# A hybrid encoder layer on one core: the values product of attention turned round in split form, the softmax division moved to GpSimd, scores two tiles ahead, and the heads' share of w_out in PSUM banks of its own

## The reference, cut to what matters

```python
# D_MODEL = 1024, SEQ = 1024, 8 heads x 64, 16 experts
x = LN(x);  proj = x @ w_in
y_hy = hyena(proj)            # 256 channels
y_lr = rglru(proj)            # 256 channels
# MLA, per head h, all 1024 queries and keys (96 = 64 nope + 32 rope channels)
s = (q_nope @ k_nope.T + q_rope @ k_rope.T) * 96 ** -0.5
p = softmax(s, axis=-1)
o = p @ v                     # 1024 x 64 per head, 8 heads: 512 channels
y = concat(rms(y_hy) * g0, rms(y_lr) * g1, rms(o) * g2)
x = LN(alpha * x + y @ w_out)
x = LN(alpha * x + expert_choice_moe(x))   # 16 experts, 128 tokens each
```

## Time and profile before

| what | value |
|---|---|
| runs (three) | 1750.42, 1754.76 (median), 1759.69 us |
| profiled execution, first to last instruction | 1750.5 us |
| busy over the span | PE 1574.6, PEld 1135.9, DVE 1075.2, ACT 757.3, POOL 247.5 us |
| attention, first scores to last values product | about 673 to 955 us |
| mix, from there to its last product | about 955 to 1070 us |
| experts | about 1131 to 1700 us |

### The profile page before, as it was taken

One profiled execution on the slowest core, in us unless ns is written; L12 is line 12 of the kernel. 1 busy time (PEld: TensorE's weight loads), 2 busy tenths in 40 slices (PEclk: granted clock), 3 DMA queues, 4 the chain that ended last, 5 costly groups with the idle time before them and its releaser, 6 DMA issues.

```text
span 1750.5 us, 18114 instructions
## 1 busy us (share of the span) xinstructions
PE 1574.6 (90%) x6806; PEld 1135.9 (65%) x6806; DVE 1075.2 (61%) x1247; ACT 757.3 (43%) x853; POOL 247.5 (14%) x140
## 2 busy tenths in 40 slices
PE   5999989999899998999998997099999999999970
PEld 2444467854334346999897786088888888888760
DVE  6211244441350436667765564779998998998858
ACT  5201100023340313445554234067777777777742
POOL 0400000000000000000000431303223322332214
PEclk9999989999999998999998997599999999999995
DMA  5506000070100000000101335779999999999964
GB/s 193 205 0 222 24 1 1 1 137 24 48 0 0 0 0 24 1 1 25 37 13 53 118 112 196 268 256 373 370 379 379 379 370 379 379 373 376 379 226 180
DMA packets 152864, 284.58 MB, mean 163 GB/s; under 512 B 25268, under 2 KB 35842, under 8 KB 152803
## 3 DMA queue, kind: packets, MB, share of 16 engines
q1 hardware_dynamic: 147043, 262.76, 42.3%
q0 software_dynamic: 4608, 16.78, 3.7%
q10 hardware_dynamic: 1152, 4.19, 0.6%
HBM read 258.54 MB, written 25.17 MB: 162 GB/s over the span
## 4 chain that ended last, share of the span: by engine, by line
PE 80%; DVE 9%; ACT 4%; DMA 4%; issue 2%; POOL 0%; POOLq 0%; ACTq 0%; SPq 0%; DVEq 0%
PE psum L936 15%; PE psum L1239 9%; PE psum L1241 8%; PE psum L1240 8%; PE psum L1126 5%; PE psum L1077 4%; PE psum L971 3%; PE psum L920 3%; DMA arena<-in_exp_w_down 3%; PE psum L1116 3%; PE psum L1185 2%; PE psum L1187 2%; PE psum L1186 2%; PE psum L981 2%; PE psum L982 2%
## 5 line engine op out<-in xcount | busy, mean ns | idle before, releaser
L1658 DVE TENSOR_TENSOR split_at<-arena,split_at 128x2048 fp32r<-128x2048 f32 x188 | 427.6, 2290 | 61.2 <-ACT split_at L819 59.5
L819 ACT ACTIVATE split_at<-arena 128x2048 fp32r<-128x2048 f32 x192 | 367.4, 1916 | 63.6 <-PE psum L1241 54.1
L1239 PE MATMUL psum<-split_at,split_at 128*128 128x512 f32 x768 | 306.2, 399 | 1.4 <-DVE split_at L1664 1.4
L1241 PE MATMUL psum<-split_at,split_at 128*128 128x512 f32 x768 | 300.7, 391 | 0.0
L1240 PE MATMUL psum<-split_at,split_at 128*128 128x512 f32 x768 | 299.8, 390 | 0.0
L936 PE MATMUL psum<-arena 128*128 128x512 f32 (+1 forms) x608 | 265.5, 596 | 3.7 <-DVE arena L1334 3.7
L936 PEld LDWEIGHTS psum<-arena 128*128 128x128 f32 (+1 forms) x608 | 113.3, 187 | 151.4 <-issue 146.8
L1241 PEld LDWEIGHTS psum<-split_at,split_at 128*128 128x128 f32 x768 | 144.7, 188 | 31.3
L1239 PEld LDWEIGHTS psum<-split_at,split_at 128*128 128x128 f32 x768 | 145.0, 189 | 29.8 <-DVE split_at L1664 1.8
L1240 PEld LDWEIGHTS psum<-split_at,split_at 128*128 128x128 f32 x768 | 145.1, 189 | 28.4
L754 ACT ACTIVATE arena<-psum,arena 128x1024 f32<-128x1024 f32 x64 | 71.2, 1113 | 134.4 <-DVE arena L1531 134.3
(11 more groups left out here) (253 smaller groups left out, 2173.2 us busy)
## 6 DMA issues: line engine op xcount, KB each, us to landing
arena<-in_exp_w_gate SPq DMA_DIRECT2D x64, 1024.0 KB, 14.2
arena<-in_exp_w_up SPq DMA_DIRECT2D x64, 1024.0 KB, 14.1
arena<-in_exp_w_down SPq DMA_DIRECT2D x64, 1024.0 KB, 14.3
arena<-in_w_in SPq DMA_DIRECT2D x9, 1024.0 KB, 5.1
arena<-in_x SPq DMA_DIRECT2D x8, 512.0 KB, 4.4
xhat_scratch<-arena SPq DMA_DIRECT2D x8, 512.0 KB, 6.5
arena<-in_w_out SPq DMA_DIRECT2D x8, 512.0 KB, 3.2
arena<-xhat_scratch SPq DMA_DIRECT2D x8, 512.0 KB, 4.8
```

What stands on the lines that cost most here:

```text
L819: a(flat(wsplit[c % WS][0]), wraw[:, c], ACT.Copy).then_inc(s_whi, 1)
L1239: mm(bank(out_bank), src[0][:, k, :], whi[:, k % 4, :], start=(k == 0), stop=False)
L1241: ins = mm(bank(out_bank), src[1][:, k, :], whi[:, k % 4, :], start=False, stop=(k == KT - 1))
L1658: tt(flat(lo), wraw[:, c], flat(hi), ALU.subtract).then_inc(s_wlo, 1)
```

## The change

Four things are changed together.

1. The values product is turned round. Two units make a pair. The turned probabilities are split (ACT copies both banks as the high part, L817; DVE subtracts, L1654) and are now the moving operand, 256 columns wide; the values, split once per head by POOL (`v_split`, high and low side by side, 128 columns), are the weights. Eight products with the high part (`pv_high`, L1225) and eight with the low part (`pv_low`, L1232) give both halves of the answer in one bank, which ACT copies (`o_copy`) and DVE adds (`o_sum`) into a transposed output. The values product is no longer followed by a turn of the outputs.
2. The division by the sum moves ahead of the turn and to POOL: DVE inverts the sum (`sum_inverse`), POOL scales the 128x1024 probabilities (L541), and `probs_turn(n)` waits for that. The subtractions for the heads, for w_out and for the two groups move from DVE to POOL too; for w_out POOL scales (L551) and subtracts (L552).
3. PE makes `scores` two units ahead of the turn, not one.
4. In the mix the heads' share goes to banks 2 and 3 and is normalised when DVE adds it; its sum of squares is made by PE from squares of ACT, four products with a column of ones per tile. The other groups' share goes to banks 0 and 1.

```diff
+            def head_low(h, part):
+
+                pool.wait_ge(s_qkh, 2 * h + 3 + part)
...
+            for n in range(N_UNIT):
+                h, qt = divmod(n, TT)
+                pool.wait_ge(s_rc, n + 1)
+                pool.tensor_scalar(p_at[:, n % 2, :], p_at[:, n % 2, :], rinv[:, n % 2:n % 2 + 1], None, ALU.mult).then_inc(s_ps, 1)
+                if h + 1 < NH and qt in (1, 3):
+                    head_low(h + 1, qt // 2)
+                if h + 1 < NH and qt == 4:
+                    v_split(h + 1)
+                if n in WOUT_AT:
+                    k = WOUT_AT.index(n)
+                    _, lo, hi = wout[k]
+                    pool.wait_ge(s_woh, k + 1)
+                    w = wout_in[:, k % 2, :]
+                    link(pool.tensor_scalar(w, w, par[:, C_GN + k:C_GN + k + 1], None, ALU.mult))
+                    pool.tensor_tensor(lo, w, hi, ALU.subtract).then_inc(s_wol, 1)
+                if n in GROUPS_AT:
...
+                    pool.wait_ge(s_yh, m + 1)
+                    pool.tensor_tensor(y_lo[g][:, c, :], (yT_hy, hs)[g][:, c, :], y_hi32[g][:, c, :], ALU.subtract).then_inc(s_yl, 1)
...
+            probs(0)
+            rotary_high(1)
+            probs(1)
             for n in range(NH * TT):
                 h, qt = divmod(n, TT)
...
+                if n >= 4 and n % 2 == 0:
+                    o_copy(n // 2 - 2)
+                probs_high(n)
+                if n + 2 < N_UNIT:
+                    probs(n + 2)
+                if h + 1 < NH and qt in (0, 2):
                     head_high(h + 1, qt // 2)
                 if n in WOUT_AT:
                     k = WOUT_AT.index(n)
                     act.wait_ge(s_wo[k % 2], 16 * (k // 2 + 1))
                     a(wout[k][0], wout_in[:, k % 2, :], ACT.Copy, scale=par[:, C_GN + k:C_GN + k + 1]).then_inc(s_woh, 1)
...
             def probs_turn(n):
-                pe.wait_ge(s_exp, n + 1)
+                pe.wait_ge(s_ps, n + 1)
...
                     if n:
-                        pe.wait_ge((s_pta, s_ptv)[b], n)
+                        pe.wait_ge(s_ptv, 2 * n + b - 1)
...
+            def pv_high(p):
+
+                h = p // 4
+                pe.wait_ge(s_pta, 2 * p + 2)
...
+                for k in range(KT):
+                    mm(bank(6 + p % 2)[:, 0:256], vs[:, h % 2, k, :], pT_hi[:, p % 2, k, :], start=(k == 0), stop=False)
...
+            for n in range(N_UNIT):
+                if n + 2 < N_UNIT:
+                    scores(n + 2)
+                probs_turn(n)
+                if n >= 2:
+                    (pv_high, pv_low)[n % 2](n // 2 - 1)
...
+            row_max(0)
+            rotary_low(1)
+            row_max(1)
+            sum_inverse(0)
+            for n in range(N_UNIT):
+                if n + 1 < N_UNIT:
+                    sum_inverse(n + 1)
+                if n + 2 < N_UNIT:
+                    row_max(n + 2)
+                if n >= 4 and n % 2 == 0:
+                    o_sum(n // 2 - 2)
+                probs_low(n)
```

More of the change, by code:

```diff
@@ L334, in encoder @@
         N_UNIT = NH * TT
-        WOUT_AT = [TT * h + qt for h in range(3, 7) for qt in (5, 7)]
-        GROUPS_AT = [N_UNIT - 7, N_UNIT - 5, N_UNIT - 3, N_UNIT - 2]
+        SUMS = 10
+        ROOTS = 3
+        N_PAIR = N_UNIT // 2
+        WOUT_AT = [TT * h + qt for h, qt in ((3, 5), (3, 7), (5, 5), (5, 7), (6, 5), (6, 7), (7, 1), (7, 3))]
+        GROUPS_AT = [TT * h + qt for h, qt in ((2, 5), (2, 7), (4, 5), (4, 7))]
         def heads_bank(u):
@@ L460, in _ @@
                 sp.wait_ge(s_acst[i], 16 * TT // 2)
-            for c in range(8, WC):
+            for c in range(7, WC):
                 load_chunk(0, c)
@@ L1171, in _, with mix @@
             pe.wait_ge(s_wol, KT)
-            y = [(group[0][:, c, :], group[1][:, c, :]) for group in (y_hy, y_lru, *y_at) for c in range(2)]
+            pe.wait_ge(s_yl, 4)
+            def mix(b0, k, high, low, first, last):
+                for j in range(2):
+                    out_, cols = bank(b0 + j), slice(HALF * j, HALF * j + HALF)
+                    mm(out_, high, wout[k][0][:, cols], start=first, stop=False)
+                    mm(out_, high, wout[k][1][:, cols], start=False, stop=False)
+                    ins = mm(out_, low, wout[k][0][:, cols], start=False, stop=last)
+                return ins
@@ new lines, in _ @@
+                    for k in range(4):
+                        ins = mix(0, k, y_hi[k // 2][:, k % 2, P * i:P * i + P], y_lo[k // 2][:, k % 2, P * i:P * i + P], k == 0, k == 3)
+                    ins.then_inc(s_mxa, 1)
+                    pe.wait_ge(s_sq, SUMS + i + 1)
+                    if i == 0:
+                        pe.wait_ge(s_ov, N_PAIR)
+                    else:
+                        pe.wait_ge(s_rsd, ROOTS + i)
+                    for c in range(4):
+                        ins = mm(bank(7)[:, i:i + 1], o_sq[:, i % 2, c, :], ones[:, 0:1], start=(c == 0), stop=(c == 3))
@@ L1188, in _ @@
+                    ins.then_inc(s_ssq, 1)
+                    pe.wait_ge(s_ol, i + 1)
+                    if i:
+                        pe.wait_ge(s_mixu, i)
+                    for c in range(4):
+                        ins = mix(2, 4 + c, ya_hi[:, i % 2, c, :], ya_lo[:, i % 2, c, :], c == 0, c == 3)
                     ins.then_inc(s_mix, 1)
@@ new lines, in sum_inverse, with probs_low @@
+                v.reciprocal(rinv[:, n % 2:n % 2 + 1], rsum[:, n % 4:n % 4 + 1]).then_inc(s_rc, 1)
+            def probs_low(n):
+                p = n // 2
+                v.wait_ge(s_pta, n + 1)
+                for b in range(2):
+                    blocks, cols = slice(4 * b, 4 * b + 4), slice(P * (n % 2), P * (n % 2) + P)
+                    tt(pT_lo[:, p % 2, blocks, cols], bank(4 + b).rearrange("p (k q) -> p k q", k=4), pT_hi32[:, p % 2, blocks, cols],
+                       ALU.subtract).then_inc(s_ptv, 1)
```

309 lines of the change are left out of this document (154 added, 155 removed).

## The result

| what | kernel before | changed kernel |
|---|---|---|
| median of the timed runs | 1757.2 us (4 runs, 1750.4 to 1759.7) | 1880.6 us (4 runs, 1879.8 to 1882.1) |
| ratio to before, 95% interval | 1 | 1.0706 (1.0681 to 1.073) |
| profiled span | 1750.5 us | 1877.8 us |
| attention, first scores to last values product | 672.93 to 954.84: 281.9 us | 676.12 to 1074.50: 398.4 us |
| from there to the first top-k instruction | 136.3 us | 144.1 us |

The change made the kernel 7% slower; 1797 us with a range of 1760 to 1838 was predicted. Of the 127.3 us between the two spans, attention has 116.5, the mix 7.9, and 3.2 are a later start of attention. The rest of the kernel is the same to 0.2 us.

What follows compares the result with a forecast made beforehand. Attention was bound by PE; afterwards POOL's in-line waits for ACT would stall PE. From 1750.5: attention +29.4, mix -5.8, clock +21.6 gave 1795.7, stated as 1797 us, range 1760 to 1838.

Steps and rivals of the forecast that it cites:

- POOL's prices: POOL in attention: a 1024-column subtraction takes 2.39 us, the scaling s = 1.2, between a fill's 0.95 and 2.39.
- POOL's own load then fits: Attention, per head: POOL's scalings, subtractions, `v_split` and up to two w_out blocks take 24 of 26 us.
- The rival that was called dear: Attention: POOL's scaling costs as much as a subtraction, 2.39, so 40 us more, 1837; chance 0.10.
- The order on POOL does not fit: Attention: side work waiting for ACT delays the next scaling; a w_out block's ring is 7.07 + 2s; stalls total 91.5 us.
- the 26 places named: Attention stalls: eight w_out blocks at 6.22 us each, four groups at 4.84, 14 next-head splits at 1.59.
- The rival that the stalls are hidden: Attention: scaling runs far enough ahead that PE does not wait; 1683 without stalls and clock loss; chance 0.14, all gains included.
- The unit without side work: Attention: a unit falls from 4.06 to 3.25 us, eight 256-column products taking 0.92; alone, 51 us less.
- the rival that 256 columns gain nothing: Attention: a 256-column product takes 0.23 us, a unit 4.17, total 1821; chance 0.05.
- the rival that DVE and POOL hold each other up: Attention: scalings slow the subtractions by 0.86 per unit, ring 4.04, 40 us more, 1837; chance 0.05.
- The mix: Stage after attention: waits of 7.3 and 5.4 us go, 6.9 for sums of squares come; net -5.8 us.
- The clock: PE in attention: half clock after each of 12 long stalls loses 1.8 us each, +21.6 us.
- The 14 short stalls I take as too short: Attention, next-head splits: these stalls were priced without clock loss; otherwise they would cost 25 us more.

Runs made afterwards that it cites:

- the run without the queue: Changed kernel with POOL's side work of unit n written behind the scaling of unit n + 2, all computation kept: 1782.8 us, 1.0147.
- the repeated scores: Changed kernel in which PE repeats its scores products in units whose turn comes late, so it has work while POOL waits: 1870.8 us, 1.0641.
- 8 columns: Changed kernel with POOL scaling only 8 of the 1024 probability columns per unit, all waits and order kept: 1798.7 us, 1.0236.

## Why the prediction was wrong

The direction and the mechanism were right, and the time was 84 us short. Against the profiled execution (1877.8, predicted 1795.7, 82.1 apart):

- **POOL's prices: this step failed.** "The scaling has one input tensor ... I take s = 1.2, near the fill": it took 2.84, above even the upper bound of 2.39. I took two inputs for the dear end because I thought the price grows with the operands. The runs show that the form of the instruction decides: 2.84 as a scaling by a column, 2.77 by a constant, 1.89 as a two-tensor product with a repeated operand, 2.34 to 2.40 for a subtraction. Why the form with fewer inputs is the dearer one stays open. The scaling stands 34 times in the stalls and once ahead of the first turn: 35 x 1.64 = 57.4 us. With the load, 8 x 2.84 + 2.40 + 2.39 + 1.9 = 29.4 us per head, "POOL's own load then fits" fell as well: it is more than PE's 26, as the run without the queue shows. The Trainium skill (GPSIMD Engine Reference, section 3.1 and section 4.1) led to estimates of 1.54 and 0.85 us; this trace agrees with neither, its 2.84 lies above both. The rival that was called dear was not dear enough.
- **The order on POOL does not fit: right.** The stalls are at the 26 places named, with the releasers named. With s = 2.84 the formula gives 7.07 + 5.68 = 12.75 for a w_out block and the trace 13.39, of which 1.09 is the turn at half clock; for the next head it gives 6.89 + 2.84 = 9.73 and the trace 873.24 - 862.83 = 10.41, with 1.10 for the half clock. The rival that the stalls are hidden did not happen. `v_split`, costed at nothing, stands on the chain in three heads; that is a small part of the rest below.
- **The unit without side work: right.** 3.21 to 3.25; 0.95 for eight products; the rival that 256 columns gain nothing is out. So is the rival that DVE and POOL hold each other up: of the changed kernel's scalings in attention none that stands alone took over 2.86, and the w_out subtractions all took 2.34. DVE's subtractions there read PSUM and SBUF; in attention the slow cases came only in the run with DVE's scaling, which reads SBUF (above).
- **The mix: wrong in sign.** -5.8 was forecast, +7.9 came, 13.7 apart. "POOL's first residual ... is done some 9 us after attention": it was, at 1080.49 + 2.40 = 1082.9, 8.4 after. The step that failed is that I looked at the first tile alone and called the rest hidden: from the second tile on POOL waits for ACT ahead of each residual, up to 11.8 us. With that order turned the stage gives -6.3, so the other parts of the term were good to 0.5 us.
- **The clock: too low, partly shown.** 21.6 was forecast as 12 times 1.8, and the step that failed here is "The 14 short stalls I take as too short". (The prediction speaks of three waits of PE and shows two.) Of the 64 turns 20 ran at half clock: the 12 behind the long stalls, 7 of the 14 behind a next head's split, as the one at 871.26 with 1.98, and the first one. On the chain these 20 have 21.9 us over 0.88 each, and the other products 13.7 over their full-clock durations, together 35.6. What attention has over the sum corrected for the scaling is 29.7 in all, 8.1 more than the forecast 21.6. The chain says that this is mostly clock; the stalls' other links were a little shorter than written down (12.30 in place of 12.75 for a block, without the half clock), and the repeated scores gave back 9.8. A finer split stays open.
- **The start: scatter.** 3.2 of the miss. The kernels of these runs have the same code up to attention and start it anywhere from 672.5 to 677.8; the kernel before starts it at 672.4. The clock ahead of it differs too:

```profile
415.00:500.00 85.00, 76.12 (x168) 0.96 0.08 25
```

```profile
415.00:500.00 85.00, 76.12 (x162) 0.92 0.08 25
```

The first row is PE in the run with the division behind the product, whose attention starts at 672.5, the second in the same kernel with the mix's order turned as well, 677.3. So 3.2 lies within the scatter of executions. The two starts go with the two clocks, but not in all runs (the changed kernel's profile has 0.92 and 675.6), so how much of the scatter is the clock's is not shown.

Sum: 57.4 + 13.7 + 8.1 + 3.2 - 0.2 = 82.2, against 82.1. The clock's 8.1 is what the other terms leave of attention, so that the closing of the sum is no proof of its parts.

The range failed by the first point: 57.4 by itself takes 1797 to 1854. A bound "from above" was drawn from an instruction that seemed to do more; nothing in the rows said that it must cost more.

## What to carry to other kernels

Before a per-unit step is given to an idle engine, put into its line all that waits for others, and follow the ring back to the unit itself; the engine's busy share says nothing of that, and even a nearly free step lost here (8 columns: 1.0236). Where the trace does not have an instruction's form on that engine, do not take another form's duration as a bound; measure it by itself first. Put work whose inputs come late behind work that others wait for, in every tile and not the first alone: that was worth 98 us in attention and 15 in the mix.

## What the runs showed of the hardware

- POOL scales 128x1024 float32 by a column of factors in 2.84 us, by a constant in 2.77; the same as a two-tensor product with one column repeated takes 1.89, a subtraction 2.34 to 2.40, 8 columns 0.31. DVE needs 0.75 undisturbed, 0.83 in the mean of the run in which it does the scaling.
- In that run POOL's w_out subtraction went from 2.34 to 2.82 us, and two of DVE's scalings, begun 0.4 us into a subtraction of POOL, took 2.56 and 2.58.
- Eight fp32r products of 256 columns take 0.95 us, 0.119 each: about half of the 0.23 of one with 512 columns.
- A turn behind repeated scores products and 3.7 us without work still ran at a granted clock of 0.50 (1.2 GHz): 1.97 us instead of 0.88. Of the changed kernel's 14 short stalls, 1.3 to 3.4 us, 7 were followed by a turn at half clock and 7 were not.
- The projection stage, the same code in all of these kernels, ran at a granted clock of 0.92 to 0.96 from one execution to the next (415 to 500 us), and the start of attention lay up to 5 us apart.
